# The first half of an output contraction as seven block products on half the tokens

## What is computed

```python
y = (o.astype(z.dtype) * jax.nn.silu(z)) @ w_out          # (512, 2048) @ (2048, 2048)
x = x + rmsnorm(y, g_post[i])
...
mem_n = rmsnorm_2(mem, mem_norm_g[l])                     # 256 memory tokens
mk = (mem_n @ w_mk).reshape(b, m, MEM_HEADS, MEM_HEAD_DIM)
mv = (mem_n @ w_mv).reshape(b, m, MEM_HEADS, MEM_HEAD_DIM)
```

## Time and profile before

| | us |
|---|---|
| runs (median of 3; lowest, highest) | 2207.74 (2207.11, 2207.95) |
| span of the profiled execution | 2207.3 |
| what lies between that span and the median | 0.4 |
| TensorE busy in the span | 2190.0 |
| VectorE, ScalarE, GpSimd busy | 1375.6, 815.8, 111.9 |
| out_product, layer 0 and layer 1, each 14 chunks | 152.3 each |
| weight load of 1 MB, issue to landing (median) | 4.9 |

### The profile page before, as it was taken

How to read it: one execution, slowest core, us unless ns; L and a number is a source line. 1 busy time by engine, 2 the same in 40 slices (tenths; PEclk the granted TensorE clock), 3 DMA queues, 4 the chain that set the end, 5 groups by cost and what they waited for, 6 DMA issues and landing times.

```text
span 2207.3 us, 27611 instructions
## 1 busy us (share of the span) xinstructions
PE 2190.0 (99%) x10348; PEld 1823.7 (83%) x10348; DVE 1375.6 (62%) x2016; ACT 815.8 (37%) x1249; POOL 111.9 (5%) x151
## 2 busy tenths in 40 slices
PE   8999999999999999999999999999999999999998
PEld 7888888888888888888888888888888888888887
DVE  6687788874248643567677732386434677677665
ACT  6433434442235421334333532345213443335221
POOL 0100001101110100000000011101000000000000
PEclk9999999999999999999999999999999999999999
DMA  7455545452247222225444432373222253435432
GB/s 280 168 157 154 163 151 159 143 186 101 97 147 268 93 96 96 76 74 158 136 140 120 167 120 95 128 272 113 98 95 74 65 158 125 144 116 159 174 118 109
DMA packets 90141, 303.05 MB, mean 137 GB/s; under 512 B 7440, under 2 KB 48656, under 8 KB 66768
## 3 DMA queue, kind: packets, MB, share of 16 engines
q1 hardware_dynamic: 83760, 270.81, 37.5%
q10 hardware_dynamic: 4896, 17.30, 2.1%
q0 software_dynamic: 1408, 13.89, 1.7%
HBM read 253.74 MB, written 48.23 MB: 137 GB/s over the span
## 4 chain that ended last, share of the span: by engine, by line
PE 95%; DVE 2%; DMA 1%; issue 1%; ACT 0%; SPq 0%; POOL 0%; DVEq 0%; POOLq 0%; ACTq 0%
PE acc L551 72%; PE sc L551 11%; PE ov L551 5%; PE ov L715 1%; PE sc L896 1%; PE sc L897 1%; PE sc L702 1%; PE sc L701 1%; DMA raw<-w_dram 1%; DMA g<-xT_dram 0%; PE acc L736 0%; PE acc L737 0%; PE acc L570 0%; PE acc L566 0%; PE acc L740 0%
## 5 line engine op out<-in xcount | busy, mean ns | idle before, releaser
L551 PE MATMUL acc<-h_hi,hi 128*128 128x512 f32 x2240 | 876.5, 391 | 8.0 <-DVE h_lo L1479 8.0
L551 PE MATMUL acc<-h_lo,hi 128*128 128x512 f32 x2240 | 873.0, 390 | 0.0
L551 PE MATMUL acc<-h_hi,lo 128*128 128x512 f32 x2240 | 872.6, 390 | 0.0
L1387 DVE TENSOR_TENSOR lo<-raw,hi 128x2048 fp32r<-128x2048 f32 (+3 forms) x178 | 390.6, 2194 | 353.1 <-ACT hi L1006 351.3
L551 PEld LDWEIGHTS acc<-h_hi,hi 128*128 128x128 f32 x2240 | 421.1, 188 | 97.7 <-issue 11.4
L551 PEld LDWEIGHTS acc<-h_hi,lo 128*128 128x128 f32 x2240 | 421.1, 188 | 88.3
L551 PEld LDWEIGHTS acc<-h_lo,hi 128*128 128x128 f32 x2240 | 421.3, 188 | 84.9
L1006 ACT ACTIVATE hi<-raw 128x2048 fp32r<-128x2048 f32 (+3 forms) x178 | 327.5, 1840 | 398.6 <-PE acc L551 256.6
L1088 ACT ACTIVATE prob<-prob,st 128x256 f32<-128x256 f32 x128 | 63.6, 498 | 109.4 <-DVE st L1540 109.4
L1020 ACT ACTIVATE sq<-acc 128x512 f32<-128x512 f32 x32 | 19.2, 600 | 224.0 <-PE acc L551 217.1
L1330 ACT ACTIVATE prob<-sc,st 128x512 f32<-128x512 f32 x64 | 44.2, 690 | 43.6 <-DVE st L1959 43.6
(11 more groups left out here) (306 smaller groups left out, 2882.6 us busy)
## 6 DMA issues: line engine op xcount, KB each, us to landing
raw<-w_dram SPq DMA_DIRECT2D x170, 1024.0 KB, 4.9
turned<-pt SPq DMA_DIRECT2D x32, 512.0 KB, 3.2
pt<-turned SPq DMA_DIRECT2D x64, 256.0 KB, 4.9
turned<-pt SPq DMA_DIRECT2D x32, 448.0 KB, 3.0
pt<-turned SPq DMA_DIRECT2D x64, 224.0 KB, 4.1
xr<-residual ACTq DMA_DIRECT2D x16, 512.0 KB, 5.1
residual<-g ACTq DMA_DIRECT2D x16, 512.0 KB, 4.7
raw<-w_dram SPq DMA_DIRECT2D x8, 896.0 KB, 6.7
```

The costliest lines, as they stand in the source:

```text
L551: ins = pe.matmul(to, a, b, start=first and n == 0, stop=last and n == 2)
L1387: dve.tensor_tensor(lo[c.slot][:, 0:width], raw[c.slot][:, 0:width], hi[c.slot][:, 0:width].bitcast(F32), ALU.subtract).then_inc(lo_done, 1)
```

## The change

The contraction of 2048 is cut in two halves of 1024 (8 tiles). Output tiles are made in pairs (`out_pair`, 7 pairs per layer, chunks c and d). The second half of the contraction is multiplied as before (`half_product`, 8 tiles, 512 columns). For the first half, weights and activations are taken as 2 x 2 blocks: weights by output tile and by even or odd tile, activations by even or odd tile and by the first or last 256 tokens. Seven block products in place of eight give the same result, with sums of blocks ahead and behind:

- GpSimd makes four sums of y blocks for each of four tile pairs m (`turned_sums`, 16 operations of 256 columns, once for each layer), ScalarE and VectorE split them (`t_hi`, `t_lo`). They stand where `m_hi` and `m_lo` will be needed.
- For each pair GpSimd makes four sums of weight blocks of 512 columns (`weight_sums`, `last_weight_sum`), in place in `raw` and in `s_two`. ScalarE and VectorE split seven units of 512 columns and two halves of 1024.
- TensorE does the seven products, each of 4 tiles x 3 matmuls of 256 columns (`block_product`), into halves of the banks 1, 2 and 3 of `sc`; three of them add to a product that is already there.
- VectorE copies seven partial results out (`fold`, 256 columns), GpSimd adds some of them (`early_fixes`, `late_fixes`, five operations of 256 columns), and VectorE adds the result to `acc` and writes `g`.
- The squares are made from `g` (`made_square`), no longer from `acc`.
- The memory tokens come in pieces of two tiles on SP's queue, are scaled and split in a small buffer, are stored to DRAM (`store_m_piece`), and are loaded back into `m_hi` and `m_lo` at the end of the stage, in four transfers of 1 MB. `memory_values(1)` waits for the first, `memory_keys(0)` for the other three. ScalarE's reloads wait for the last store.
- The angle operations are spread over the pairs 1 to 5 of layer 0, between the scaling of a memory piece and its low part.
- The host packs the weights of the pairs by blocks.

```diff
+    SP_, SU, TW = KT // 2, 512, 2048
+    T_ORDER = ((2, 3, 0, 1), (0, 3, 1, 2))
+    T_EARLY = (3, 2)
```

SyncE's queue, in `w2`'s part of the program:

```diff
+                load_m_piece(0)
+                store_m_piece(0)
+                load_m_piece(1)
+                for q in range(1, NP):
+                    load2(WO + 2 * q + 2)
+                    load2(WO + 2 * q + 3)
+                    store_m_piece(q)
+                    load_m_piece(q + 1)
+                load2(MEMORY, width=MW[0])
+                load2(MEMORY + 1, width=MW[1])
+                store_m_piece(NP)
+                sp.wait_ge(chunk_done, pair_of(l, NP)[0].n + 1)
+                for n, at in enumerate((1, 0, 2, 3)):
+                    to, src = (x.rearrange("p (s k n) -> p s k n", s=2, k=4)[:, :, at] for x in (m_all[:, :].bitcast(F32), m_parts))
+                    sp.dma_start(to, src).then_inc(m_rest_in if n else m_first_in, 16)
```

GpSimd (`c, d, no` are the two chunks of a pair and its number):

```diff
+            def weight_sums(l, q):
+                pool.wait_ge(loaded[c.slot], (c.uses + 1) * 16)
+                if q > 1:
+                    pool.wait_ge(unit_lo, (no - 1) * 6 + 4)
+                pool.tensor_tensor(s1, w[:, A21], w[:, A22], ALU.add).then_inc(s_sum, 1)
+                pool.wait_ge(s_sum, no * 4 + 1)
+                pool.tensor_tensor(s2, s1, w[:, A11], ALU.subtract).then_inc(s_sum, 1)
+                pool.tensor_tensor(w[:, A21], w[:, A11], w[:, A21], ALU.subtract).then_inc(s_sum, 1)
...
+                if l == 0:
+                    pool.wait_ge(y1, KT // 2 + 1)
+                    pool.wait_ge(kcur_done, PAIRS * 3)
+                    pool.wait_ge(scores1, PAIRS + 1)
+                    turned_sums(l, 0)
+                    pool.wait_ge(vcur_done, PAIRS * 2)
+                    pool.wait_ge(shift1, PAIRS * 2)
+                    turned_sums(l, 1)
+                    pool.wait_ge(turned1, PAIRS * 2)
+                    turned_sums(l, 2)
+                    weight_sums(l, 1)
+                    pool.wait_ge(values1, PAIRS + 1)
+                    turned_sums(l, 3)
...
+                for q in range(1, SP_):
+                    early_fixes(no)
+                    if q == 1:
+                        add_first_squares(sqacc, sq_no(l, POSTN))
+                    else:
+                        for t in (2 * q - 2, 2 * q - 1):
+                            add_square(sqacc, t + sq_no(l, POSTN), t % 2)
+                    if q < NP:
+                        weight_sums(l, q + 1)
+                    late_fixes(no)
+                    if q < NP:
+                        last_weight_sum(l, q + 1)
```

TensorE:

```diff
+            def block_product(c, bank_, unit, src, first, last):
+                for m in range(4):
+                    both = src(m)
+                    w = slice(unit.start + m * P, unit.start + (m + 1) * P)
+                    to, high_, low_ = bank(bank_, TILES), hi[c.slot][:, w], lo[c.slot][:, w]
+                    pe.matmul(to, high_, both[:, 0, :], start=first and m == 0, stop=False, skip_group_check=True)
+                    pe.matmul(to, high_, both[:, 1, :], start=False, stop=False, skip_group_check=True)
+                    ins = pe.matmul(to, low_, both[:, 0, :], start=False, stop=last and m == 3, skip_group_check=True)
+                return ins
...
+            def out_pair(l, q):
+                pe.wait_ge(unit_lo, no * 6 + 3)
+                if q > 1:
+                    pe.wait_ge(folded, no * 7 - 2)
+                block_product(c, 1, UNIT[0], y_block(0, 0), True, False).then_inc(product_done, 1)
+                pe.wait_ge(unit_lo, no * 6 + 4)
+                pe.wait_ge(t_low, l * 4 + 4)
+                if q > 1:
+                    pe.wait_ge(folded, no * 7)
+                block_product(c, 2, UNIT[1], t_block(1), True, False).then_inc(product_done, 1)
+                block_product(c, 3, UNIT[2], t_block(0), True, False).then_inc(product_done, 1)
+                pe.wait_ge(half_lo, no + 1)
+                pe.wait_ge(evacuated[c.slot], c.accs)
+                half_product(d, 0, acc[c.slot][:, :]).then_inc(half_done, 1)
+                pe.wait_ge(folded, no * 7 + 2)
+                block_product(c, 2, UNIT[3], t_block(2), False, False).then_inc(product_done, 1)
+                pe.wait_ge(unit_lo, no * 6 + 6)
+                pe.wait_ge(folded, no * 7 + 3)
+                block_product(c, 1, UNIT[2], y_block(1, 0), False, True).then_inc(product_done, 1)
+                block_product(c, 3, UNIT[0], y_block(1, 1), False, True).then_inc(product_done, 1)
+                pe.wait_ge(lo_done, c.n + 1)
+                pe.wait_ge(folded, no * 7 + 4)
+                block_product(c, 2, UNIT[1], t_block(3), False, True).then_inc(chunk_done, 1)
+                pe.wait_ge(lo_done, d.n + 1)
+                pe.wait_ge(evacuated[d.slot], d.accs)
+                half_product(d, 1, acc[d.slot][:, :]).then_inc(chunk_done, 1)
...
-                pe.wait_ge(m_done, l * ODD + ODD)
+                pe.wait_ge(m_first_in, l * 16 + 16)
                 memory_values(1)
                 sums(added, sq_no(l, PREN) + 2)
+                pe.wait_ge(m_rest_in, l * 48 + 48)
```

ScalarE, the early token sums, the first units of the next pair, and the reloads:

```diff
+            def t_hi(l, n):
+                m = T_ORDER[l][n]
+                act.wait_ge(t_sum, (l * 4 + n) * 4 + 4)
+                act.activation(t_part(t_parts, m)[:, :, 0, :], t_part(t_raw, m)[:, :, 1, :], ACT.Copy).then_inc(t_high, 1)
+
+            for n in range(T_EARLY[0]):
+                t_hi(0, n)
             for t in (A, B):
                 act.wait_ge(y1, t + 2)
                 y_hi_tile(t)
...
+            def first_units(l, q):
+                act.wait_ge(s_sum, no * 4 + 3)
+                if q > 1:
+                    act.wait_ge(product_done, (no - 1) * 6 + 4)
+                unit_high(c, UNIT[3], w[:, A21], unit_hi)
...
-                act.wait_ge(m_done, l * ODD + ODD)
+                act.wait_ge(m_part_out, (l + 1) * ODD * 32)
                 for w in range(XR):
                     reload_residual(l, w)
```

VectorE:

```diff
+            def fold(to, b):
+                dve.tensor_copy(to, bank(b, TILES)).then_inc(folded, 1)
...
+            for n in range(T_EARLY[0]):
+                t_lo(0, n)
             y_first(B)
             for t in (A, B):
                 y_lo_tile(t, t + 1)
...
+            def out_pair(l, q):
+                dve.wait_ge(product_done, no * 6 + 1)
+                if no > 0:
+                    dve.wait_ge(fixes, no * 5)
+                fold(p1[:, :], 1)
+                dve.wait_ge(product_done, no * 6 + 2)
+                fold(p16[:, :], 2)
+                unit_low(c, UNIT[0], w[:, A11], no * 6 + 5, unit_lo)
+                dve.wait_ge(product_done, no * 6 + 3)
+                fold(p15[:, :], 3)
+                unit_low(c, UNIT[2], w[:, A12], no * 6 + 6, unit_lo)
+                unit_low(c, UNIT[1], w[:, A22], None, lo_done)
+                half_low(d, 1, no)
+                m_normed_piece(l, q)
+                if l == 0:
+                    angles(q)
+                m_lo_piece(l, q)
+                dve.wait_ge(product_done, no * 6 + 4)
+                fold(fix[1][:, TILES:S], 2)
+                dve.wait_ge(product_done, no * 6 + 5)
+                fold(fix[0][:, 0:TILES], 1)
+                if more:
+                    first_unit_lows(l, q + 1, 0)
+                dve.wait_ge(product_done, no * 6 + 6)
+                fold(fix[0][:, TILES:S], 3)
+                if more:
+                    first_unit_lows(l, q + 1, 1)
+                    first_unit_lows(l, q + 1, 2)
+                dve.wait_ge(chunk_done, c.n + 1)
+                fold(fix[1][:, 0:TILES], 2)
+                if more:
+                    first_unit_lows(l, q + 1, 3)
+                dve.wait_ge(half_done, no + 1)
+                dve.wait_ge(folded, no * 7 + 7)
+                dve.wait_ge(fixes, no * 5 + 4)
+                dve.tensor_tensor(g[:, tile(2 * q)], acc[c.slot][:, :], fix[0][:, :], ALU.add).then_inc(evacuated[c.slot], 1)
...
```

More of the change, by code:

```diff
@@ L158, in build @@
         m0 = free[0]
[L159 removed]
+        m_all = sb("m_all", 2 * KT * MEM, F32R)
+        m_hi, m_lo = m_all[:, 0:KT * MEM], m_all[:, KT * MEM:2 * KT * MEM]
         m1 = m0 + 4 * KT * MEM
         a0 = free[0]
[L163 removed]
+        free[0] += 4 * 4096
         c0 = free[0]
@@ new lines, in y_block, with t_block, half_product @@
+            def y_block(odd, tokens):
+                both = h_all[:, :].rearrange("p (s t h n) -> p s t h n", s=2, t=KT, h=2)
+                return lambda m: both[:, :, 2 * m + odd, tokens, :]
+            def t_block(j):
+                return lambda m: t_part(t_parts, m)[:, j]
+            def half_product(d, n, to):
+                for k in range(KT // 2, KT):
+                    w, x = slice(HALF[n].start + (k - KT // 2) * P, HALF[n].start + (k - KT // 2 + 1) * P), tile(k)
+                    ins = passes(to, hi[d.slot][:, w], lo[d.slot][:, w], h_hi[:, x], h_lo[:, x], k == KT // 2, k == KT - 1)
+                return ins
@@ L768, in out_product @@
             def out_product(l):
```

(34 more changed lines are left out.)

261 lines of the change are left out of this document (207 added, 54 removed).

## The result

The changed kernel takes 2244.99 us (median of 4 runs, 2242.19 to 2248.57), the kernel before 2207.76: 1.017 times as long, 95% interval 1.0156 to 1.0184. The forecast of slower was right; the time is 23 us above the predicted one and 7 above the range.

A forecast was written before the change was run, and what follows sets the result against it. TensorE was taken to bound the kernel, busy 2190.0 of 2207.3 us at full clock. Terms -11.2 + 8.4 + 8 + 2 + 7 = +14.2 us gave 2221.5, forecast 2222 us; range 2201 to 2238, the forecast's own 2212 to 2235.

The forecast's parts named there:

- The saving on columns: TensorE in the seven pairs of both layers: 0.80 us less per pair, 11.2 us saved over 14 pairs.
- Waits inside pairs: TensorE waiting for low parts or copies within the pairs: 8.4 us lost (0 to 19), 0.6 per pair.
- The lengthening by exclusion: GpSimd and two-SBUF-input VectorE operations exclude each other, so their work adds up to 19.7 of a pair's 20.96 us.
- my chain from buffer to low part: Buffer free, load, GpSimd sums, low part for the next pair's first product: 2.3 us early, or 1.3 late with exclusion.
- the other place I named: Copy of product four, queued on VectorE behind memory pieces and angle operations, holds the seventh product 0.5 us.
- Entry of layer 0: Token sums, weight sums and low parts delay the last y tiles: 8 us lost (1.2 to 10).
- Entry of layer 1: Early token work, weight sums and later token sums meeting VectorE's last low parts: 2 us lost (0 to 4).
- The memory parts: TensorE waits for 4 MB of memory pieces loaded back from DRAM: 7 us lost (4.8 to 18), 3.5 per layer.
- my bound of 9 us per layer: Memory parts' most per layer: last store starts transfers 2 us late, 1.5 MB of residual reloads take 4.5 us in shared queues.
- Rival 3: The pair loop becomes the bound, 22.3 us or more per pair: 2238 us and above; chance 0.12.
- Rival 1: The GpSimd-VectorE port costs nothing on the path: 2198 to 2203, say 2200 us, faster; chance 0.21.

The follow-up runs named there:

- Run 9: Changed kernel with reworked memory pieces, angles at pair ends, first pair left as plain full products, three token blocks made after h_all's last tile: 2209.05 us, 1.001.
- run 10: Run 9's kernel with the angle operations spread over the first three pairs and the last memory piece made right behind product three: 2206.09 us, 0.9994.
- Run 4: Changed kernel with layer 0's angle operations moved to the end of each pair on VectorE: 2242.53 us, 1.0164.
- Run 6: Changed kernel with GpSimd's token sums made on 2 of 256 columns, parts split from g instead, weight sums kept: 2238.11 us, 1.0137.
- Run 3: Changed kernel with one turned token block's parts instead of two ahead of layer 1's last y tile on ScalarE and VectorE: 2247.77 us, 1.018.
- run 5: Changed kernel with GpSimd making layer 1's second turned token block before the first pair's weight sums: 2244.03 us, 1.0173.
- run 1: Changed kernel with ScalarE's three residual reloads held until the memory pieces have landed, in both layers: 2234.77 us, 1.0118.
- run 7: Changed kernel with memory pieces reordered, token blocks reversed, two transfers started earlier, and residual reloads held until the pieces landed: 2227.75 us, 1.0091.
- run 11: Kernel before the change, plus one wait per layer: memory_keys(0) starts only after a 1 MB copy inside DRAM lands: 2232.86 us, 1.0111.

## Why the prediction was wrong in size

- **The saving on columns** held: 0.76 us per pair instead of 0.80 (a pair of 21.00, not 20.96 us), 10.6 instead of 11.2 us. Layer 1 in runs 9 and 10 shows it undisturbed.
- **Waits inside pairs**, 8.4 (0 to 19): 6.3 us, slow matmuls included, 5.2 of them in layer 0. The lengthening by exclusion is there (the 70 low parts of 512 columns made from `raw` take 1.08 us in the mean instead of 0.68), but my chain from buffer to low part was late in no pair: no pair's first product waits. What waited was the other place I named, the copy of product four behind angles and memory piece (0.6 and 2.4 us), and once a low part (0.5 us). Run 4 shows that the angles are half of it.
- **Entry of layer 0**, 8 (1.2 to 10): 8.1 us. The size is right, and as far as the rows go the mechanism too. I gave 1.2 us to VectorE's three low parts and the rest to GpSimd's turns. Run 6 gives GpSimd's token sums 2.6 us, and its rows put 2.7 us of VectorE's lateness on the weight sums. I had no term for the half clock: 1.7 us of this entry are such matmuls (472.5 to 475.9 us). That the weight sums cost this much is read from rows and not shown by a run without them.
- **Entry of layer 1**, 2 (0 to 4): 7.9 us. This step failed. I called the early work "ahead of a value tile that TensorE delivers late anyway" and did not follow the two token blocks back through ScalarE to GpSimd's queue, where the second stands behind sums that wait for a weight chunk (landed at 1269 us). Runs 3 and 5 show that reordering alone moves the wait to the second product: sums, parts and the last y tiles want VectorE and GpSimd at once. Run 9, which gives them the time of a plain pair, leaves 1.5 us.
- **The memory parts**, 7 (4.8 to 18): 20.4 us, above the upper end and the largest miss. I put 4 MB alone at 12.3 us and took a value near the lower end. Beside the reloads and the weight chunks the last piece landed 13.5 us behind the stretch, not 7.3. Late store and shared queues were in my bound of 9 us per layer, which the half clock behind the wait then passed; run 1 prices the reloads at 3.6 us a layer, as bytes do, and run 7 removes the rest.
- **The clock** had no term at all. Behind or between TensorE's waits, in five places, the matmuls ran at 1.2 GHz for some microseconds: about 10 us in sum, and run 11 shows it by itself. Without it the changed kernel would have stood at about 2235 us, inside the range. Either this term or the memory parts' right size would have kept the result in it. The two overlap: the sizes measured above contain the half clock of their stretches.

So the steps that failed are the size of the memory parts, the wait at the entry of layer 1, and the half clock put at nothing. The waits inside pairs came out 2.1 us below their term and the saving 0.6 us below its own, which changes little. Rival 3 had the right time by another mechanism, which did not occur: the pair loop was not the bound. Rival 1's port cost nothing in eleven pairs, but it did in pair 2 of layer 0 and in the entries. Not tried: leaving the weight sums out, at the entries or within the pairs, leaving out the fixes, and how much of layer 0's entry is the clock alone.

## What to carry to other kernels

When TensorE is full, price every wait twice: its length, and the matmuls that may run at half clock behind it. For an early job put in front of a critical one, follow its inputs back through every in-order queue that they pass, and price it in the stretch where it runs; a saving that needs preparation is cheapest if one unit of the old work is kept as cover for it. A transfer that ends a stage shares its rate with everything that becomes free to start at the same moment: count those bytes too, or hold them back.

## What the runs showed of the hardware

- **A wait of 2 to 3 us may cost the clock or not.** Behind the 2.4 us wait in pair 2 of layer 0 it did (1.5 us over 24 of the matmuls that follow). In two executions with waits of 2.65 and 3.94 us at the last y tiles of layer 0, those of the changed kernel and of run 1, the windows around and behind them were:

```profile
486.00:492.00 6.00, 4.07 (x18) 3.39 (x19) 4.70 (x5) 1.15 (x3) 1.04 (x2) 1.00 0.14 20
492.00:498.00 6.00, 6.00 (x30) 5.03 (x29) 4.81 (x6) 3.59 (x7) 2.14 (x2) 1.00 0.50 198
```
```profile
486.00:492.00 6.00, 3.37 (x8) 2.69 (x9) 5.37 (x6) 0.63 (x1) 1.01 (x1) 0.62 0.00 0
492.00:498.00 6.00, 6.00 (x23) 4.81 (x23) 1.51 (x3) 3.21 (x7) 0.00 (x0) 0.81 0.65 218
```

  The entry took 3.3 us more in the second. In the first the clock had been at half 13 us earlier, from 472.5 to 475.9 us, behind waits of 0.8, 0.2, 1.3 and 0.2 us; in the second it stayed at 1.00 there. The kernels with waits also spread more from run to run (run 4: 2235.9 to 2247.9 us, at mean clocks of 0.994 to 0.990) than the kernel before (2206.4 to 2209.9 over all its runs here). One wait lies far from every edit, in layer 1's heads: it is 0.7 us in the changed kernel (at 1817.5 us), and 1.8 to 2.0 us with half clock behind it in the profiled executions of runs 3, 5, 6, 7 and 11, which makes them some 2.5 us longer. Single differences of that size between two profiled executions show little.
- **One sum of GpSimd took 5.20 us instead of 1.29** (L597's row above, at 1269.27 us) while VectorE ran four two-input operations end to end. Beside the low parts of run 5, where the two engines took turns, the same sum took 1.65. The Trainium skill (SBUF — State Buffer, Who interferes with whom) has the shared port pair as an exclusive lock that one instruction holds to its end; the rows agree, and show besides that GpSimd can miss three turns in a row.
- **The reloads on ScalarE's queue took their share from SyncE's transfers** though they were issued 5 us later (queue shares of 21.7 and 68.5% above). The Trainium skill (DMA: Bandwidth & Descriptors, Queues, rings and completion order) says that a DMA engine goes round the queue rows that have work, packet by packet; run 1's 3.6 us agree with it.
